# Two neighbouring rows of the down weights per partition, in a mixture-of-experts block

## What is computed

```python
def expert_block(args):
    xb, e = args
    gu = xb @ w_gu[e] + b_gu[e]
    gate, lin = gu[:, :D_EXPERT], gu[:, D_EXPERT:]
    gate = jnp.minimum(gate, SWIGLU_LIMIT)
    lin = jnp.clip(lin, -SWIGLU_LIMIT, SWIGLU_LIMIT)
    act = (lin + 1.0) * (gate * jax.nn.sigmoid(SWIGLU_ALPHA * gate))
    return act @ w_down[e] + b_down[e]
```

## Time and profile before

| | |
|---|---|
| median of 3 runs | 1746.84 us (1746.36 to 1748.47) |
| the profiled execution | 1746.15 us |
| its span, first to last instruction | 1744.3 us |
| TensorE matmul busy | 1647.6 us (94%) |
| TensorE weight loads busy (beside the matmuls) | 1373.1 us (79%) |
| VectorE, ScalarE, GpSimd busy | 62%, 48%, 8% |
| mean granted TensorE clock | 0.973 of full |
| HBM traffic | 273 GB/s over the span, about 367 in the loop |

### The profile page before, as it was taken

How to read it: one execution, slowest core, us unless ns; L and a number is a source line. 1 busy time by engine, 2 the same in 40 slices (tenths; PEclk the granted TensorE clock), 3 DMA queues, 4 the chain that set the end, 5 groups by cost and what they waited for, 6 DMA issues and landing times.

```text
span 1744.3 us, 26775 instructions
## 1 busy us (share of the span) xinstructions
PE 1647.6 (94%) x9998; PEld 1373.1 (79%) x9998; DVE 1075.8 (62%) x1139; ACT 831.2 (48%) x844; POOL 134.8 (8%) x220
## 2 busy tenths in 40 slices
PE   6999989999966799999999999999999999999994
PEld 5876657987745688888888888888888888888882
DVE  4221553434255677777777777776777767777773
ACT  4243364434221455555546555455455554555543
POOL 0020220000000000100001000010000100001001
PEclk9999999999977899999999999999999999999997
DMA  5111123422065799999999999999999999999965
GB/s 201 49 49 49 48 97 121 145 82 79 24 261 203 240 361 365 384 364 370 369 371 373 365 375 365 368 386 369 360 371 372 375 374 365 369 370 377 364 247 162
DMA packets 134773, 477.05 MB, mean 273 GB/s; under 512 B 10242, under 2 KB 10291, under 8 KB 134707
## 3 DMA queue, kind: packets, MB, share of 16 engines
q1 hardware_dynamic: 123968, 446.72, 68.6%
q0 software_dynamic: 7168, 25.17, 6.2%
q10 hardware_dynamic: 3602, 4.69, 0.8%
HBM read 457.67 MB, written 18.87 MB: 273 GB/s over the span
## 4 chain that ended last, share of the span: by engine, by line
PE 90%; DVE 4%; ACT 3%; DMA 2%; issue 1%; ACTq 0%; SPq 0%; POOL 0%; DVEq 0%; POOLq 0%
PE psum L977 23%; PE psum L996 21%; PE psum L1019 21%; PE psum L609 17%; PE psum L788 1%; PE psum L777 1%; PE psum L971 1%; PE psum L963 1%; PE psum L765 1%; PE psum L880 1%; PE psum L900 1%; ACT ring_split L1116 1%; PE psum L914 0%; DVE ring_split L1496 0%; DMA X<-in_x 0%
## 5 line engine op out<-in xcount | busy, mean ns | idle before, releaser
L977 PEld LDWEIGHTS psum<-MIX,ring 128*128 128x128 f32 x4096 | 774.9, 190 | 100.9 <-DVE MIX L1904 0.9
L977 PE MATMUL psum<-MIX,ring 128*128 128x96 f32 x4096 | 725.6, 259 | 0.2 <-DVE MIX L1904 0.2
L1871 DVE TENSOR_TENSOR ring_split<-ring,w_hi_a 128x2048 fp32r<-128x2048 f32 x64 | 146.5, 2289 | 88.4 <-ACT w_hi_a L1363 86.6
L1877 DVE TENSOR_TENSOR ring_split<-ring,w_hi_x 128x2048 fp32r<-128x2048 f32 x64 | 146.5, 2288 | 88.3 <-ACT w_hi_x L1372 88.3
L996 PE MATMUL psum<-ring_split,xs_hi 128*96 128x512 f32 x512 | 200.3, 437 | 0.0
L1019 PE MATMUL psum<-ring_split,act_hi 128*96 128x512 f32 x512 | 199.0, 436 | 0.0
L1871 DVE TENSOR_TENSOR ring_split<-ring,w_hi_x 128x2048 fp32r<-128x2048 f32 x64 | 146.4, 2289 | 74.2 <-ACT w_hi_x L1363 74.2
L609 PE MATMUL psum<-ring_split,H_hi 128*128 128x512 f32 (+1 forms) x512 | 151.8, 380 | 0.6 <-DVE ring L1582 0.6
L1877 DVE TENSOR_TENSOR ring_split<-ring,w_hi_a 128x2048 fp32r<-128x2048 f32 x64 | 146.2, 2285 | 3.5 <-ACT w_hi_a L1372 3.5
L1372 ACT ACTIVATE w_hi_a<-ring 128x2048 fp32r<-128x2048 f32 x64 | 121.7, 1901 | 7.0 <-DMA ring<-in_w_down 7.0
L1372 ACT ACTIVATE w_hi_x<-ring 128x2048 fp32r<-128x2048 f32 x64 | 121.8, 1904 | 2.6 <-DMA ring<-in_w_down 2.6
(11 more groups left out here) (284 smaller groups left out, 2647.1 us busy)
## 6 DMA issues: line engine op xcount, KB each, us to landing
ring<-in_w_gu SPq DMA_DIRECT2D x256, 1024.0 KB, 10.2
ring<-in_w_down SPq DMA_DIRECT2D x128, 1024.0 KB, 12.1
ring<-in_w_in SPq DMA_DIRECT2D x6, 2048.0 KB, 10.5
X<-in_x SPq DMA_DIRECT2D x8, 512.0 KB, 7.9
ring<-in_w_out SPq DMA_DIRECT2D x2, 2048.0 KB, 7.7
ring<-in_w_mk SPq DMA_DIRECT2D x2, 2048.0 KB, 9.0
ring<-in_w_mv SPq DMA_DIRECT2D x2, 2048.0 KB, 7.8
ring<-in_w_mq SPq DMA_DIRECT2D x2, 2048.0 KB, 7.7
```

The costliest lines, as they stand in the source:

```text
L977: return mm(psum[:, dst, q * C:(q + 1) * C], lhsT=gate_w(k // 2)[:, k % 2, f * P:(f + 1) * P], rhs=xsT[:, k, :], start=k == 0 and q == 0, ...
L1871: v.tensor_tensor(lin_lo(c), lin_w(c), chunk_hi(c).bitcast(F32), ALU.subtract)\
L1877: v.tensor_tensor(down_lo(c), down_w(c), chunk_hi(c).bitcast(F32), ALU.subtract)\
```

## The change

The rows of a down chunk are dealt to the partitions in pairs: partition p gets rows 2p and 2p + 1, 8 KB that lie together in HBM and in the ring. So position k = 0 of the chunk holds the even rows and k = 1 the odd ones. Hidden block f must then hold the even or odd units of its 256: `hidden_cols(f)` is a slice of 128 columns with a step of two. The gate block's weights, the rows that are transposed and the bias take it. Loads of `w_gu`, the number of instructions, their shapes and all waits stay.

```diff
         def down_rows(e, c):
-            return w_down[0, e, 256 * c:256 * c + 256, :].rearrange("(k p) c -> p k c", p=P)
+            return w_down[0, e, 256 * c:256 * c + 256, :].rearrange("(p k) c -> p k c", p=P)
+
+        def hidden_cols(f, a=0):
+
+            start = a + 256 * (f // 2) + f % 2
+            return slice(start, start + 2 * P - 1, 2)
...
             for f in range(16):
-                last = nc.tensor.transpose(b[:, f * E:(f + 1) * E], bgu_rows[:, f * P:(f + 1) * P],
+                last = nc.tensor.transpose(b[:, f * E:(f + 1) * E], bgu_rows[:, hidden_cols(f % 8, D * (f // 8))],
                                            ident[0:32, 0:32])
...
                     last = nc.tensor.transpose(psum[:, T0 + f // 4, (f % 4) * C:(f % 4 + 1) * C],
-                                               lin_rows[:, f * P:(f + 1) * P], ident[0:C, 0:C])
+                                               lin_rows[:, hidden_cols(f)], ident[0:C, 0:C])
...
-                return mm(psum[:, dst, q * C:(q + 1) * C], lhsT=gate_w(k // 2)[:, k % 2, f * P:(f + 1) * P],
+                return mm(psum[:, dst, q * C:(q + 1) * C], lhsT=gate_w(k // 2)[:, k % 2, hidden_cols(f)],
```

## The result

The changed kernel takes 1778.94 us, the median of five runs (1776.16 to 1779.76), against 1746.84 us before. The ratio is 1.0178, with a 95% interval of 1.0164 to 1.0192: 32 us or 1.8% slower. I had forecast 1746.7 us.

The account below looks back on a forecast made before the run. TensorE was taken to bound the kernel, with thin reserve in the loads. The terms, 0 + 0 + 0 - 0.1 us on the median of 1746.84, gave 1746.7 us; the range ran from 1741 to 1762 us, with 0.82.

Parts of the forecast that it names:

- The down transfers: Load queue, 128 transfers of 1 MB: merging 4 KB pieces into 8 KB saves 14 ns each, hidden in slack: nothing.
- b_gu's queue: Only load with 8 KB pieces, at most 610 ns each: up to 262 ns more per merged piece, 8.4 us per item.
- Nothing is merged: Rival: the engines still cut the down transfers at 4 KB; same time, 1746.8 us; chance 0.08.
- the loads become the bound: Rival: 8 KB pieces take over about 22 ns more than 348; 1774 us at 50 ns over, up to 1997; chance 0.05.
- The gate columns: Line 977's 4096 weight loads, now read with a step of two: taken as nothing, bounds 0 to 434 us.
- the moving rate: Moving operands of 512 columns run at 0.23 us, 8.9 bytes per ns: about what stepped gate loads would need.
- The transposes: Lines 971 (256) and 678 (16), their loads read with a step of two: taken as nothing, upper bound 15.2 us.
- only the transposes slow down: Rival: stepped loads slow on lines 971 and 678 alone; up to 1762 us, 1754 at half; chance 0.05.
- The biases: Gate and linear biases pass through the same 16 transposes of line 678, one copy per item; no wait added.
- The tail: Last item's down chunk 2, a 5.04 us transfer open on the path: eight merges per engine save 0.11 us.
- The faster rival: Rival at the kernel's end: open transfer 2.7 us sooner and half clock not granted, together 5.3 us, 1741.5; chance 0.05.
- slow weight loads: Rival: line 977's step-two loads take twice as long, 217 us more, 1964 us, up to 2180; chance 0.13.

## Why the prediction was wrong

**What bounds the kernel**: right. TensorE filled the loop before and after, and an item's growth is in its instructions.

**The down transfers**: right in the result. Merged as forecast (16,385 packets fewer against 16,384), nothing of it on the path. The gain per piece was below the 14 ns I carried over from 2 KB packets: 5 ns, or 0.16 us per item instead of 0.45. The price from b_gu's queue was indeed mostly sharing. "Nothing is merged" and "the loads become the bound" are both refuted.

**The gate columns**: the step that failed. I wrote "I take nothing, by the nearest row, the moving rate". It is worth 17.5 us by the run with that edit alone. The bounds, 0 and 434 us, held it, and the 217 us of its rival were 12 times too much, because I doubled the load's whole time per column. How a slower load reaches the chain was right: the first of a block's two hides and the second doesn't (118 ns more on the loads at a step of four gave 120 ns more behind the block). The nearest row wasn't the right one: a moving operand of 512 columns reads plain lines, four floats from each, and says how many bytes per ns are read, not how many lines. It was also short by its own numbers, 8.9 bytes per ns where the sweep needed 9.6. What the runs put in its place is a load that takes the longer of 0.83 ns per column and 1.75 ns per line. At a step of two that is 112 ns against 106. The two are so near each other that the price is 6 ns per load, and the next step up costs ten times that.

The Trainium skill's rule in "SBUF — State Buffer", section "Door 1: The DMA port swizzle", stood between two readings. For the gate loads its first half is nearly borne out, as two hits per line cost 6 ns of 190, and with one hit per line the penalty it speaks of is there, 118 ns. The figure of four floats that the same paragraph gives as a stride for free doesn't hold: with four the kernel took 266 us more, of which the transposes are some 8.

**The transposes**: the second term that was mis-sized, from nothing to 8.4 us by the run with it alone, inside its bounds of 0 and 15.2. I had said that I took it with less trust; it is the rival "only the transposes slow down" at just above its half price, but not alone. The loads, at 222 ns, even passed the 196 ns that I gave as the most, while the chain took 0.26 us more and not the 0.45 of that bound: a recorded load that overlaps the one ahead of it is no measure of the cost.

**The biases**: the 16 transposes went once from 1.1 to 2.0 us, from the first of them to the matmul behind the last, 0.9 us that I had folded into the transposes' bound.

**The tail**: the open transfer took 4.72 us after, 4.80 with the pieces alone and 5.04 before. That doesn't show the gain of 0.1 us that I put into the sum: in runs with the old pieces the same transfer took 4.99 (gate step alone), 4.84 (transposes' step alone) and 4.86 us (all steps). The faster rival's price was nearly right: 5.3 us forecast, 5.9 measured. But it isn't reached by a faster transfer; it took two changes of order, and the pieces don't bring it.

**The chances and the range**: slower had 0.23, and 0.13 of it was for slow weight loads at 217 us and more. I priced that rival at its upper bound only and left it out of the range whole. An unknown with bounds of 0 and 434 us has a middle, and a small share of it, 6 ns of 190 on 4096 loads, is already outside 0.2%.

**What stays open.** The loop explains 28 of the 32 us and the biases 0.9. The other 3 us lie ahead of the loop: in the profiled executions the first gate load comes at 552.0 us against 547.1 before, the biases included. Up to 4 us of such a delay needs no change at all: in the runs with steps of eight, four and three, whose code ahead of the loop is that of the kernel before, it came at 548.6, 549.3 and 551.2 us (the lines above). TensorE's clock is reduced in other slices there (the PEclk line above, against the one in the earlier trace rows). What sets that, and whether the changed kernel meets the late case more often, wasn't settled. And the transposes don't follow the rate by lines: 64 lines would make 196 ns, which is their minimum, but the median is 222, and 128 lines, twice as many, leave it at 218. The first of each eight, which starts beside a 512-column matmul, takes 199 ns at a step of two and 201 at four; the others start 120 ns apart at both. Why they pay about one price for any step was not found.

## What to carry to other kernels

Ask of a layout change which operand pays for it. Here bigger pieces relieved the DMA engines, which nobody waited for, and the bill went to 4096 weight loads on the engine that sets the end; 6 ns on each were 1% of the kernel. Where an index must be stepped, a copy on an engine with room may take the step: ScalarE took that of the transposes for twice its 1 us at no cost.

An unknown that multiplies thousands of instructions on the bounding engine has no harmless size, so its range belongs in the forecast's range. And look at a tail instruction by instruction: the order of three pieces of work there was worth 5.9 us, where the forecast had 0.1 us for the change.

## What the runs showed of the hardware

- A float32 weight load of 128 columns takes 190, 196, 252, 308 and 321 ns at steps of one, two, three, four and eight floats: 84 ns plus the longer of 0.83 ns per column and 1.75 ns per 16-byte line, to within 1 ns up to four (eight lies 13 ns above).
- The loads of transposes take 140 ns plain and 222, 208, 218 and 209 ns at steps of two, three, four and eight, and eight transposes in a row 0.66 us plain and 0.92, 0.88, 0.92 and 0.86 us: about one price for any step.
- A slower weight load counts only where its partner is short. The matmul behind a block waited 7 ns longer for loads 6 ns longer, and 120 ns longer for loads 118 ns longer; the first matmul of a block, with 512 columns ahead of it, came 2 to 3 ns later in both cases.
- ScalarE's copy of 96 x 1024 floats out of PSUM takes 1.02 us, and 2.01 us when it writes them in turn to two groups of 128.
